# The first loads of a hybrid layer: x in two transfers of 64 partitions a half, from SyncE and ACT, and the first norm's weights from GpSimd

## The reference

```python
def rms_norm(x, gain):
    xf = x.astype(jnp.float32)
    y = xf * lax.rsqrt(jnp.mean(xf * xf, axis=-1, keepdims=True) + EPS)
    return (y * gain.astype(jnp.float32)).astype(x.dtype)
...
h = rms_norm(x, attn_norm[l])
p = h @ w_in[l]
aq, ak, av, hq, hf, hi, hg = jnp.split(p, SPLIT_POINTS, axis=-1)
attn_out = sliding_window_attention(aq, ak, av, q_norm[l], k_norm[l], attn_sinks[l])
hg_out = hgrn2(hq, hf, hi, hg, lower_bounds[l], hg_norm[l])
x = x + jnp.concatenate([attn_out, hg_out], axis=-1) @ w_out[l]
h = rms_norm(x, ffn_norm[l])
x = x + conv_ffn(h, w_ffn_up[l], ffn_conv_w[l], ffn_conv_b[l], w_ffn_down[l])
```

## Time and profile before

| | |
|---|---|
| median of 3 runs | 1083.03 us (1083.01 to 1083.12) |
| the profiled execution | 1083.67 us |
| its span, first to last instruction | 1081.9 us |
| PE busy in the span | 1076.5 us |
| DVE, ACT, POOL busy | 908.9, 631.5, 72.0 us |
| moved by DMA | 249.08 MB |

### The profile page before, as it was taken

The page is one execution under the profiler, slowest core; times in us unless marked ns, Lnnn a source line. Parts: engine busy times, 40 slices in busy tenths (PEclk is TensorE's granted clock), DMA queues, the critical chain, the costliest instruction groups (busy, mean ns, idle before and its releaser), DMA issues.

```text
span 1081.9 us, 18172 instructions
## 1 busy us (share of the span) xinstructions
PE 1076.5 (100%) x6549; PEld 930.6 (86%) x6549; DVE 908.9 (84%) x1371; ACT 631.5 (58%) x925; POOL 72.0 (7%) x100
## 2 busy tenths in 40 slices
PE   9999999999999999999999999999999999999998
PEld 8888888888888888888888888888898888888887
DVE  6877988889656578888888888887877899999997
ACT  6677666757544655545555555545555566656663
POOL 4500000000000000000000000000000000000000
PEclk9999999999999999999999999999999999999999
DMA  7645677777788968788787878888887877887782
GB/s 262 195 139 154 194 203 228 193 243 203 225 234 259 258 216 245 222 237 218 247 228 233 237 208 256 229 232 239 245 233 223 236 260 263 282 279 254 287 313 95
DMA packets 185070, 249.08 MB, mean 230 GB/s; under 512 B 9125, under 2 KB 143158, under 8 KB 184758
## 3 DMA queue, kind: packets, MB, share of 16 engines
q1 hardware_dynamic: 170118, 212.30, 60.6%
q0 software_dynamic: 12480, 31.46, 15.2%
q10 hardware_dynamic: 2416, 4.60, 1.2%
HBM read 243.75 MB, written 36.04 MB: 259 GB/s over the span
## 4 chain that ended last, share of the span: by engine, by line
PE 98%; DMA 1%; DVE 1%; ACT 0%; issue 0%; SPq 0%; DVEq 0%; ACTq 0%
PE bank L1769 38%; PE bank L1777 20%; PE bank L2154 7%; PE bank L2153 7%; PE bank L2152 7%; PE bank L2005 3%; PE bank L1837 3%; PE bank L1839 3%; PE bank L1838 3%; PE bank L2006 3%; PE bank L2007 3%; PE bank L1739 1%; DMA xt<-in_x_dram 1%; PE bank L2044 0%; PE bank L1924 0%; PE bank L1814 0%
## 5 line engine op out<-in xcount | busy, mean ns | idle before, releaser
L758 ACT CAST w_hi<-raw 128x1024 fp32r<-128x1024 f32 x299 | 313.1, 1051 | 254.8 <-PE bank L1777 122.7
L1161 DVE TENSOR_TENSOR w_lo<-raw,w_hi 128x1024 fp32r<-128x1024 f32 x299 | 363.9, 1222 | 107.7 <-ACT w_hi L758 107.2
L1769 PE MATMUL bank<-hs,w_hi 128*128 128x512 f32 x1792 | 423.0, 391 | 0.0
L1769 PEld LDWEIGHTS bank<-hs,w_hi 128*128 128x128 f32 x1792 | 331.2, 188 | 66.3 <-issue 0.9
L1777 PEld LDWEIGHTS bank<-hs,w_lo 128*128 128x128 f32 x1792 | 224.6, 191 | 5.7 <-issue 0.2
L1777 PE MATMUL bank<-hs,w_lo 128*128 128x256 f32 x1792 | 227.3, 283 | 0.0
L1131 ACT CAST hi_slot<-slot 128x1024 fp32r<-128x1024 f32 (+1 forms) x96 | 110.9, 1188 | 68.5 <-DVE slot L1696 37.3
L1680 DVE TENSOR_TENSOR slot_lo<-slot,hi_slot 128x1024 fp32r<-128x1024 f32 (+1 forms) x96 | 128.7, 1387 | 4.5 <-ACT hi_slot L1131 3.6
L2154 PE MATMUL bank<-hi_slot,gated 128*128 128x512 f32 (+1 forms) x202 | 78.2, 387 | 0.0
L2152 PE MATMUL bank<-hi_slot,gated 128*128 128x512 f32 (+1 forms) x202 | 78.2, 387 | 0.0
L1598 DVE SCALAR_TENSOR_TENSOR C<-U,cols,C 128x256 f32<-128x256 f32 x176 | 73.4, 479 | 0.0
(11 more groups left out here) (249 smaller groups left out, 1197.8 us busy)
## 6 DMA issues: line engine op xcount, KB each, us to landing
raw<-in_w_ffn_up_dram SPq DMA_DIRECT2D x176, 512.0 KB, 4.8
u_sums<-in_w_ffn_down_dram POOLq DMA_DIRECT2D x60, 512.0 KB, 6.7
raw<-in_w_in_dram SPq DMA_DIRECT2D x52, 512.0 KB, 4.6
slot<-in_w_ffn_down_dram SPq DMA_DIRECT2D x36, 512.0 KB, 4.8
raw<-in_w_in_dram SPq DMA_DIRECT2D x64, 256.0 KB, 3.3
raw<-in_w_out_dram SPq DMA_DIRECT2D x32, 512.0 KB, 5.1
slot<-u_sums SPq DMA_DIRECT2D x60, 256.0 KB, 5.6
slot<-in_w_ffn_down_dram SPq DMA_DIRECT2D x30, 256.0 KB, 4.1
```

The lines of the kernel that those rows point to most:

```text
L758: act.copy(w_hi[:, i, :], raw[:, i, :]).then_inc(units_hi, 1)
L1161: dve.tensor_tensor(w_lo[:, i, :], raw[:, i, :], w_hi[:, i, :].bitcast(F32), ALU.subtract)\
L1769: m = pe.matmul(banks[b][:, :], w_hi[:, i, c], hs[:, 4 * i + k, :], start=(first and k == 0), stop=(final and k == 3))
```

## The change

The gains of the first norm go from ACT's queue to GpSimd's, ahead of everything else that GpSimd does after raising some counters. Each half of x is split by partitions: SyncE issues partitions 0 to 63 of half 0, then of half 1; ACT issues partitions 64 to 127 of half 0, then of half 1, then the second norm's gains as before. PE waits for 32 instead of 16 on each half's semaphore. In the changed file the lines stand 1 to 3 lower.

```diff
+X_SPLIT = 64
...
             for t in range(TT):
-                sp.dma_start(xt[:, t, :], x_v[:, t, :]).then_inc(x_loaded[t], 16)
+                sp.dma_start(xt[0:X_SPLIT, t, :], x_v[0:X_SPLIT, t, :]).then_inc(x_loaded[t], 16)
...
             for s in (st_made, ab_made):
                 pool.sem_inc(s, FREE)
+            pool.dma_start(rows[0:KT, 0, :], attn_norm.rearrange("a (r c) -> (a r) c", c=P))\
+                .then_inc(gains_loaded, 16)
             pool.memset(ident[:, :], 0.0).then_inc(setup_step, 1)
...
-            act.dma_start(rows[0:KT, 0, :], attn_norm.rearrange("a (r c) -> (a r) c", c=P))\
-                .then_inc(gains_loaded, 16)
+            for t in range(TT):
+                act.dma_start(xt[X_SPLIT:P, t, :], x_v[X_SPLIT:P, t, :]).then_inc(x_loaded[t], 16)
             act.dma_start(rows[KT:2 * KT, 0, :], ffn_norm.rearrange("a (r c) -> (a r) c", c=P))\
                 .then_inc(second_gains_loaded, 16)
...
-            pe.wait_ge(x_loaded[0], 16)
+            pe.wait_ge(x_loaded[0], 32)
...
-            pe.wait_ge(x_loaded[1], 16)
+            pe.wait_ge(x_loaded[1], 32)
```

## The result

| | before | after |
|---|---|---|
| median, lowest to highest (us) | 1083.07, 1083.01 to 1083.12 (6 runs) | 1090.92, 1090.42 to 1091.19 (6 runs) |
| the profiled execution, its span (us) | 1083.67, 1081.9 | 1090.42, 1088.7 |
| ratio, 95% interval | | 1.0072 (1.0062 to 1.0082) |

The change costs 7.85 us, 0.7%. The forecast was 0.1 us less than before, in a range of 1082.5 to 1087.6: wrong in direction, and outside the range.

The account below looks back on a forecast made before the run. PE was taken to bound the kernel, leaving an earlier x at most 0.28 us. Terms -0.25 (start of x), +0.15 (interleaving), 0 and 0 gave -0.1 on the median 1083.03: 1082.9 us, range 1082.5 to 1087.6.

Parts of the forecast that it names:

- What bounds the start: PE, busy nearly throughout, carries a shift of the start to the end; an earlier x gives at most 0.28 us.
- I take the value near the lower end, by the row at 1.00 busy: Loading x by 64 partitions: busy DMA engines should mostly serve different halves, so only half a packet is lost, +0.15 us.
- the interleaving: Cost of two queues' 64-partition transfers of x running side by side: 0 to 4.3 us (5.3 with the first microsecond).
- The evenly mixed halves: While x loads, engines draw from two queues and should be on different partition halves most of the time.
- Rival A: Loading x: 64 partitions take half the rate and engines serve the same half together; +4.3 us, 1087.3; chance 0.28.
- Its sign, that PE waits for x: At the start, 200 to 264 GB/s from 3 to 8 us and PE waiting for x 2 us or more.
- Rival C: The two queues of x are served unevenly, so half 0 lands late; 1083.3 or 1084.6 us; chance 0.09.
- By size it is nearest to ACT's row, so I take 3.8: GpSimd's gains should land 3.8 us after issue plus 0.4 for the issue, at 5.0: cost 0.
- The upper end of 8.4: Latest landing of GpSimd's gains, from its slowest 512 KB transfer at 7.6 us; up to +2.4 us.
- Rival B: GpSimd's gains land after 8.1 us and PE turns them late; up to +2.4 us, 1085.4; chance 0.05.
- The clock: PE's granted clock, 2.4 GHz throughout; if it fell while PE stood idle it would cost more, no size given.
- The split's other terms: Work queued behind the new issues (weight unit, table load, second gains, masks, parameter rows) has slack: 0.

Follow-up runs that it names:

- run 2: The changed kernel with the first norm's gains put back at the head of ACT's queue, so only the split by partitions stays; 1087.54 us, +3.95.
- run 4: The kernel before with x as four transfers of 64 partitions, all from SyncE's one queue, gains still from ACT; 1087.94 us, +4.35.
- run 5: The kernel before with x in six SyncE transfers: partitions 32 to 95 of both halves, then 0 to 31, then 96 to 127; 1088.16 us, +5.0.
- run 3: The changed kernel with each half of x split by columns instead of partitions over SyncE and ACT, gains still from GpSimd; 1087.50 us, +3.9.
- run 1: The kernel before with only the first norm's gains moved from ACT to GpSimd, x unsplit from SyncE; 1086.06 us, +2.5.
- run 10: The changed kernel with 33 instead of 10 idle matmuls on PE ahead of its wait for the gains; 1088.32 us.
- run 7: The kernel before with x split by columns over SyncE and ACT, gains at the head of ACT's queue; 1084.89 us, +1.8.
- run 9: The kernel before, all from SyncE except ACT's gains: first columns of both halves, first weight unit, other columns; PE's order changed to match; 1083.66 us, +0.6.

## Why the prediction was wrong

**What bounds the start.** This step held. What was lost lies ahead of PE's second unit, 6.7 of 6.8 us, and reached the end one for one. The other side of it, that at most 0.28 us can be gained, stays untested: no version was faster.

**"I take the value near the lower end, by the row at 1.00 busy."** This step failed first. It priced the interleaving at +0.15 us within bounds of 0 and 4.3; alone it measured +3.95 (run 2). The row says that the 16 DMA engines are occupied. They are occupied just as much, 0.92 to 1.06, while they move 209 to 219 GB/s. The evenly mixed halves that I counted on did not come about: the queues took turns in blocks. Rival A had the rate and the price (about 210 GB/s; 4.3 us, against 3.95 and 4.35 in runs 2 and 4), and its chance of 0.28 was too low. Its sign, that PE waits for x, did not show in the changed kernel, since the gains came later still; it showed in runs 2, 4 and 5. Rival C, queues served unevenly, came about as well, but together with the low rate, so its own price can't be read.

The Trainium skill, "SBUF — State Buffer", in "Can I just issue two DMAs to hit both halves?", has two such transfers only 6% faster than one; with its 196 GB/s for 64 partitions the prediction had worked out 208 GB/s and, as an estimate, +4.8 us. The trace agrees, with 207 to 250. With its further sentence, that only one transfer over all 128 partitions reaches all the ports, it does not agree: run 5 streams partitions 32 to 95 at 419 GB/s. "DMA: Bandwidth & Descriptors", "Rules for kernel authors", gives the same advice for another reason, that the halves share the same engines. By run 3, where two queues share them at full rate, that reason is not the one that counts here.

**"By size it is nearest to ACT's row, so I take 3.8."** This failed as well, and so did the bound above it. The issue began at 1.75, not 0.8; the landing took 5.7 us with x at full rate and 9.8 with the halved one. The upper end of 8.4 came from GpSimd's 512 KB transfers far behind the start, where the core moved 231 GB/s on average; the trace of before has no row for a small transfer of GpSimd behind the stream of x. Rival B had a chance of 0.05 and 2.4 us; in the changed kernel it is what PE waits for. That B's 2.4 is so near to the +2.5 of run 1 is luck: the gains landed there at 7.43, worth 1.6 us by B's own sum, and the rest was PE's clock.

**The rivals were kept apart.** This is why the range failed: A and B were priced singly, but what makes A also makes B worse: the split by partitions moved the gains' landing from 7.4 (run 1) or 7.7 (run 3) to 11.6. With PE at work throughout (run 10) the loss is 5.3 us, 1088.3 by its median: outside the range even without the clock, and more than B's 2.4 or the 4.3 of A that the range took in.

**The clock.** The text said of it only that it could cost more if it fell. It did, and no term of the sum stood for it: 2.6 us between the changed kernel and run 10, which also contains that run's better pace in the idle matmuls behind the gains, 0.94 us against 1.53 before.

**The split's other terms,** ACT's table load, the second gains, GpSimd's masks and SyncE's rows, cost nothing that shows: in run 10 PE waits for the gains (0.53 us) and otherwise only where it had waited before. Its start is 4.8 us later than before, though, and that gave them time.

**What stays open:** why the queues take turns in blocks when split by partitions, but mix when split by columns; whether the halved rate comes from the partitions written or from the rows read; why the first 4 KB of each row of x stream at 188 to 228 GB/s when they are asked for first (runs 7 and 9) and at 422 together with the rest (run 3); why PE's first matmuls run at 6 to 7 records in a us, against 11 later (run 10), under a clock column of 1.00 for both; and what holds GpSimd's 8 KB back behind the slow stream. No run separates these.

## What to carry to other kernels

Before a transfer is split by partitions, look first at which partitions each part covers: here 0 to 63 and 64 to 127 had about 210 GB/s each, 32 to 95 had 419. The number of queues did not set that rate, but it did move the landings. A DMA share of 1.00 proves neither full rate nor that nothing can get worse; read it beside the GB/s. And when small inputs gate the start, price them behind the stream as the change will leave it, and rivals together, for one delay can lengthen the other.

## What the runs showed that I had not expected

- A transfer over partitions 32 to 95 is as fast as one over all 128 (419 against 424 GB/s in the same stretch), one over 0 to 31 or 96 to 127 as slow as one over 64 at an end (210 against 215).
- Two issues at the same moment from two queues were served one after the other: their parts of half 0 landed 4.9 and 7.3 us after issue (the changed kernel).
- A GpSimd transfer of 8 KB took 5.7 us to land beside a stream at 428 GB/s and 9.8 beside one near 210; the same transfer at the head of ACT's queue took 1.6 (run 2) to 3.8 (before).
- PE's granted clock fell to 0.50 after it had been idle since 5.4 us, was there from 9 to 15 us, and the work after the wait ran slower for it; 23 more idle matmuls gave back 2.6 us.
